# Rescheduling sparse expert visits and building part of the one-hot rows on ScalarE in a PEER encoder layer

## What is computed

```python
q = (ht @ w_q).reshape(T, PEER_HEADS, 2, PEER_HALF)          # 8 heads, two halves
s = jnp.einsum('thpd,hpnd->thpn', q, sub_keys)               # 128 keys for each half
... top 16 of 16 x 16 pairs for each head -> experts, gates  # 128 experts of 16,384 for each token
a = jax.nn.gelu(jnp.einsum('td,tkd->tk', xt, u[e]))
y = jnp.einsum('tk,tkd->td', g * a, v[e])
```

## Time and profile before

| | us |
|---|---|
| median of three runs (lowest to highest) | 2524.3 (2521.87 to 2529.54) |
| the profiled execution | 2519.59 |
| its span, first to last instruction | 2517.8 |
| PE busy | 2389.7 (95%) |
| DVE busy | 1828.6 (73%) |
| POOL busy | 1332.9 (53%) |
| ScalarE busy | 927.4 (37%) |

### The profile page before, as it was taken

The page is one execution under the profiler, slowest core; times in us unless marked ns, Lnnn a source line. Parts: engine busy times, 40 slices in busy tenths (PEclk is TensorE's granted clock), DMA queues, the critical chain, the costliest instruction groups (busy, mean ns, idle before and its releaser), DMA issues.

```text
span 2517.8 us, 34594 instructions
## 1 busy us (share of the span) xinstructions
PE 2389.7 (95%) x12777; PEld 2033.9 (81%) x12777; DVE 1828.6 (73%) x3571; ACT 927.4 (37%) x1426; POOL 1332.9 (53%) x892
## 2 busy tenths in 40 slices
PE   7988999999999898899999999899799999999997
PEld 7868999999866667788888888687688788878786
DVE  4673796454378788659897298597597688888886
ACT  4443444654333322333333333233233333333333
POOL 0000698000466674564444367588586388888860
PEclk9987999999999899999999999999999999999999
DMA  5433677877766665573444478978978899999994
GB/s 166 156 130 123 206 223 221 262 218 229 241 199 213 196 219 201 198 254 117 139 150 138 149 244 259 349 237 261 362 243 275 315 332 344 347 348 347 341 369 161
DMA packets 252679, 596.84 MB, mean 237 GB/s; under 512 B 35792, under 2 KB 118224, under 8 KB 251872
## 3 DMA queue, kind: packets, MB, share of 16 engines
q1 hardware_dynamic: 182496, 385.69, 45.8%
q0 software_dynamic: 67712, 201.61, 23.9%
q10 hardware_dynamic: 2304, 7.34, 0.9%
HBM read 521.12 MB, written 73.40 MB: 236 GB/s over the span
## 4 chain that ended last, share of the span: by engine, by line
PE 35%; POOL 17%; issue 4%; DMA 4%; DVE 4%; ACT 2%; SPq 1%; DVEq 0%; ACTq 0%
PE ps L805 28%; POOL a_got L478 9%; POOL picked L473 8%; PE ps L835 3%; DMA raw<-in_experts 3%; PE ps L1051 2%; DMA picked<-in_experts,vidx 1%; SPq L358 1%; DVE acc L1534 1%; DVE acc_odd L1534 1%; PE ps L1024 1%; POOL sp_lo L469 0%; PE ps L851 0%; ACT sp_hi L691 0%; DVE att L1317 0%
## 5 line engine op out<-in xcount | busy, mean ns | idle before, releaser
L473 POOL DMA_INDIRECT picked<-in_experts,vidx x384 | 517.7, 1348 | 542.6 <-PE ps L805 219.4
L805 PE MATMUL ps<-ht_hi,sp_hi 128*128 128x256 f32 (+1 forms) x2048 | 701.4, 342 | 17.4 <-DVE sp_lo L1583 14.4
L805 PE MATMUL ps<-ht_lo,sp_hi 128*128 128x256 f32 (+1 forms) x2048 | 690.4, 337 | 0.0
L805 PE MATMUL ps<-ht_hi,sp_lo 128*128 128x256 f32 (+1 forms) x2048 | 689.7, 337 | 0.0
L478 POOL DMA_INDIRECT a_got<-acts,aidx x384 | 514.9, 1341 | 127.5 <-issue 116.1
L469 POOL TENSOR_TENSOR sp_lo<-raw,sp_hi 128x1024 fp32r<-128x1024 f32 x112 | 296.9, 2666 | 453.0 <-ACT sp_hi L691 453.0
L805 PEld LDWEIGHTS ps<-ht_hi,sp_hi 128*128 128x128 f32 x2048 | 390.1, 190 | 61.4 <-DVE sp_lo L1583 19.1
L805 PEld LDWEIGHTS ps<-ht_hi,sp_lo 128*128 128x128 f32 x2048 | 389.5, 190 | 40.7
L805 PEld LDWEIGHTS ps<-ht_lo,sp_hi 128*128 128x128 f32 x2048 | 390.2, 191 | 36.4
L1583 DVE TENSOR_TENSOR sp_lo<-raw,sp_hi 128x1024 fp32r<-128x1024 f32 x144 | 176.3, 1224 | 223.1 <-ACT sp_hi L691 222.8
L699 ACT ACTIVATE act_g<-ps 128x256 f32<-128x256 f32 (+1 forms) x256 | 125.8, 491 | 527.2 <-PE ps L805 525.3
(11 more groups left out here) (187 smaller groups left out, 3608.2 us busy)
## 6 DMA issues: line engine op xcount, KB each, us to landing
raw<-in_experts SPq DMA_DIRECT2D x256, 512.0 KB, 3.9
v_raw<-in_experts SPq DMA_DIRECT2D x128, 512.0 KB, 5.9
raw<-in_front SPq DMA_DIRECT2D x104, 512.0 KB, 3.7
acts<-act_g SPq DMA_DIRECT2D x128, 256.0 KB, 3.3
act_in<-acts SPq DMA_DIRECT2D x128, 192.0 KB, 5.9
acts<-act_g SPq DMA_DIRECT2D x128, 128.0 KB, 2.2
gates<-stage SPq DMA_DIRECT2D x16, 1024.0 KB, 11.4
g_in<-gates SPq DMA_DIRECT2D x128, 128.0 KB, 5.9
```

Of the source, the lines that this page charges most:

```text
L473: pool.indirect_dma_start(picked[n % SLOTS][:, :], None, v_rows, bass.IndirectOffsetOnAxis(ap=vidx[:, n // P, n % P:n % P + 1], axis=0)).t ...
L805: last = pe.matmul(out, l, r, start=start and k == 0, stop=stop and k == 2, skip_group_check=True)
```

## The change

Four edits. ScalarE builds `hot_a` of each second group with two activations for each token, |iota - key| and then relu(gate - gate * that), which is the gate where the key matches and 0 elsewhere; PE waits for them with `hot_a_ready`. The list `weight` becomes 23 ahead of a gate step, 4 in a store step and 17 in others. The remainders of steps 181 to 183 go from POOL to DVE, and so the spread of visits begins at step 181. For a fourth row in `idx_t` (minus the gate) some buffers of the last phase get other addresses.

```diff
+TOP_K_END = N_KEYS + 53
...
-        idx_t = sb("idx_t", A0 + 16 * KB, [P, 3, SPARSE, P])
+        idx_t = sb("idx_t", A0 + 16 * KB, [P, 4, SPARSE, P])
...
-            if step < 56 or N_KEYS <= step < N_KEYS + 56:
+            if step < 56 or N_KEYS <= step < TOP_K_END:
                 by_pool[step] = len(by_pool) + 1
...
+            def hot_rows(t, g):
+
+                n = 32 * (t - SPARSE) + g
+                if n >= HOT:
+                    act.wait_ge(S["gate_mm"], n - HOT + 1)
+                act.wait_ge(S["idx_ready"], t - SPARSE + 1)
+                for k in range(4):
+                    tok = 4 * g + k
+                    last = act.activation(hot_a[:, g % HOT, k, :], s["iota"][:, :], ACT.Abs, scale=-1.0,
+                                          bias=idx_t[:, 0, t - SPARSE, tok:tok + 1])
+                last.then_inc(S["hot_dist"], 1)
+                act.wait_ge(S["hot_dist"], n // 2 + 1)
+                for k in range(4):
+                    tok = 4 * g + k
+                    last = act.activation(hot_a[:, g % HOT, k, :], hot_a[:, g % HOT, k, :], ACT.Relu,
+                                          scale=idx_t[:, 3, t - SPARSE, tok:tok + 1],
+                                          bias=idx_t[:, 2, t - SPARSE, tok:tok + 1])
+                last.then_inc(S["hot_a_ready"], 1)
...
                 gelu(step)
                 if step + 2 < STEPS:
                     u_hi(step + 2)
+                window = gate_window(step + 1)
+                if window:
+                    hot_rows(window[0], window[1] + 1)
...
                 pe.wait_ge(S["hot_ready"], n + 1)
+                if g % 2:
+                    pe.wait_ge(S["hot_a_ready"], n // 2 + 1)
...
-                dve.tensor_copy(idx_t[:, :, t - SPARSE, :], ps[:, 6, 0:3 * P].rearrange("p (c n) -> p c n", c=3)
-                                ).then_inc(S["idx_ready"], 1)
+                dve.tensor_copy(idx_t[:, 0:3, t - SPARSE, :], ps[:, 6, 0:3 * P].rearrange("p (c n) -> p c n", c=3))
+                dve.tensor_scalar(idx_t[:, 3, t - SPARSE, :], ps[:, 6, 2 * P:3 * P], -1.0, None, ALU.mult
+                                  ).then_inc(S["idx_ready"], 1)
...
-                for q in range(4):
-                    tok = 4 * g + q
-                    last = dve.tensor_scalar(hot_a[:, g % HOT, q, :], s["iota"][:, :], idx_t[:, 0, t - SPARSE, tok:tok + 1],
-                                             idx_t[:, 2, t - SPARSE, tok:tok + 1], ALU.is_equal, ALU.mult)
+                if g % 2 == 0:
+                    for q in range(4):
+                        tok = 4 * g + q
+                        last = dve.tensor_scalar(hot_a[:, g % HOT, q, :], s["iota"][:, :],
+                                                 idx_t[:, 0, t - SPARSE, tok:tok + 1],
+                                                 idx_t[:, 2, t - SPARSE, tok:tok + 1], ALU.is_equal, ALU.mult)
...
-            u_parts(N_KEYS + 56)
-            first_free = N_KEYS + 56
-            weight = [11 if gate_window(step + 1) else 8 for step in range(first_free, STEPS)]
+            u_parts(TOP_K_END)
+            first_free = TOP_K_END
+
+            def stores(step):
+                return any(0 <= step - GATES_AT[t] - GATE_ROWS < PARTS for t in DENSE[:-1])
+
+            weight = [23 if gate_window(step + 1) else 4 if stores(step) else 17 for step in range(first_free, STEPS)]
```

More of the change, by code:

```diff
@@ L181, in encoder_program @@
                   for i, at in enumerate((0, 4 * KB, 8 * KB, 12 * KB, V0 + 19 * KB + 512))]
-        v_raw = sb("v_raw", A0 + 32 * KB, [P, RING, 1024])
+        v_raw = [sb(f"v_raw{k}", A0 + at * KB, [P, 1024]) for k, at in enumerate((32, 36, 44, 28))]
         v_hi = [sb(f"v_hi{k}", A0 + at * KB, [P, 1024], F32R) for k, at in enumerate((0, 4, 48))]
         v_lo = [sb(f"v_lo{k}", A0 + at * KB, [P, 1024], F32R) for k, at in enumerate((8, 12, 60))]
-        act_in = [sb(f"act_in{k}", A0 + at * 512, [P, HALF]) for k, at in enumerate((42, 45, 112, 115))]
-        g_in = sb("g_in", A0 + 52 * KB, [P, RING, 2 * P])
+        act_in = [sb(f"act_in{k}", A0 + at * 512, [P, HALF]) for k, at in enumerate((104, 107, 112, 115))]
+        g_in = [sb(f"g_in{k}", A0 + at * KB, [P, 2 * P]) for k, at in enumerate((22, 23, 40, 41))]
         w_f = sb("w_f", 16 * KB, [P, 2, HALF])
@@ L210, in encoder_program @@
             "dve_step", "pool_step", "sc_done", "evac", "tk_first", "tk_second", "tk_diff", "tk_exp",
-            "tk_chosen", "idx_turned", "idx_ready", "hot_ready",
+            "tk_chosen", "idx_turned", "idx_ready", "hot_ready", "hot_dist", "hot_a_ready",
             "gate_mm", "gate_evac", "gate_out3", "gate_out4", "fg_in",
@@ L376, in load_v @@
             def load_v(r):
-                sp.dma_start(v_raw[:, r % RING, :], a["experts"][r, 1]).then_inc(v_in[r % RING], 16)
+                sp.dma_start(v_raw[r % RING][:, :], a["experts"][r, 1]).then_inc(v_in[r % RING], 16)
             def load_weights(r):
                 sp.dma_start(act_in[r % RING][:, :], acts_rows[1][r, :, P:]).then_inc(act_in_done[r % RING], 16)
-                sp.dma_start(g_in[:, r % RING, :], a["gates"][r, :, SPARSE * P:(NT - 1) * P]
+                sp.dma_start(g_in[r % RING][:, :], a["gates"][r, :, SPARSE * P:(NT - 1) * P]
                              ).then_inc(gate_in[r % RING], 16)
@@ L708, in v_part @@
                     act.wait_ge(S["y_done"], r - 2)
-                act.activation(v_hi[r % 3][:, :], v_raw[:, r % RING], ACT.Copy).then_inc(S["v_hi"], 1)
+                act.activation(v_hi[r % 3][:, :], v_raw[r % RING][:, :], ACT.Copy).then_inc(S["v_hi"], 1)
             def exponents(step):
@@ L1496, in hot @@
                     dve.wait_ge(S["gate_mm"], n - HOT + 1)
-                dve.tensor_tensor(hot_b[:, g % HOT], s["iota"][:, None, :].broadcast_to([P, 4, P]),
-                                  idx_t[:, 1, t - SPARSE, 4 * g:4 * g + 4, None].broadcast_to([P, 4, P]), ALU.is_equal)
-                for q in range(4):
-                    tok = 4 * g + q
-                    last = dve.tensor_scalar(hot_a[:, g % HOT, q, :], s["iota"][:, :], idx_t[:, 0, t - SPARSE, tok:tok + 1],
-                                             idx_t[:, 2, t - SPARSE, tok:tok + 1], ALU.is_equal, ALU.mult)
+                last = dve.tensor_tensor(hot_b[:, g % HOT], s["iota"][:, None, :].broadcast_to([P, 4, P]),
+                                         idx_t[:, 1, t - SPARSE, 4 * g:4 * g + 4, None].broadcast_to([P, 4, P]),
+                                         ALU.is_equal)
+                if g % 2 == 0:
[4 more added lines that the diff above has]
+                                                 idx_t[:, 2, t - SPARSE, tok:tok + 1], ALU.is_equal, ALU.mult)
                 last.then_inc(S["hot_ready"], 1)
@@ L1559, in weights @@
                 dve.tensor_tensor(w_f[:, r % 2, 2 * P:], act_in[r % RING][:, 2 * P:], stage[:, r, :], ALU.mult)
-                dve.tensor_tensor(w_f[:, r % 2, 0:2 * P], act_in[r % RING][:, 0:2 * P], g_in[:, r % RING], ALU.mult
+                dve.tensor_tensor(w_f[:, r % 2, 0:2 * P], act_in[r % RING][:, 0:2 * P], g_in[r % RING][:, :], ALU.mult
                                   ).then_inc(S["w_ready"], 1)
@@ L1573, in v_part @@
                     dve.wait_ge(S["a_done"], STEPS)
-                dve.tensor_tensor(v_lo[r % 3][:, :], v_raw[:, r % RING], v_hi[r % 3][:, :].bitcast(F32), ALU.subtract
+                dve.tensor_tensor(v_lo[r % 3][:, :], v_raw[r % RING][:, :], v_hi[r % 3][:, :].bitcast(F32), ALU.subtract
                                   ).then_inc(S["v_lo"], 1)
@@ L1658, in _ @@
                     u_parts(step + 1)
-                    hot(t, first)
+                    if step >= GATES_AT[SPARSE]:
+                        hot(t, first)
                     visits(min(share, 1))
-                    hot(t, first + 1)
+                    if step >= GATES_AT[SPARSE]:
+                        hot(t, first + 1)
                     visits(max(share - 1, 0))
```

## The result

| us | before | after |
|---|---|---|
| median of four runs (lowest to highest) | 2526.92 (2521.87 to 2534.59) | 2558.93 (2555.72 to 2559.49) |
| the profiled execution, its span | 2519.59, 2517.8 | 2558.72, 2556.9 |

The ratio is 1.0109 [1.008, 1.0138], so the kernel after is about 1% slower. The two profiled executions differ by 39.1 us, where the sum of the prediction gave 22.2.

The account below looks back on a forecast made before the run. PE was taken to set the pace in undisturbed stretches, with full DMA engines stalling store steps. The profiled 2519.6 - 35.4 + 57.6 gave 2541.8 us; from the median, 2524.3 + 22.2, about 2546 us, range 2513 to 2572.

Parts of the forecast that it names:

- ScalarE's late start: Gate steps: PE waits 1.2 us for ScalarE's rows in each of 48 steps, 57.6 us (33 to 68); chance 0.62.
- The chain: Gelu, rounding, four Abs, own wait, four Relu: reaches PE 3.89 to 4.62 us after the Gelu, wanted at +3.20.
- the upper bound: ScalarE's chain with extra operand at 0.113 us and SBUF read at 0.034: ends at 4.62 us, late by 1.42.
- the own wait: On ScalarE, between the Abs and the Relu: Relu waits 0.09 us for the engine's own semaphore.
- The win from the spread: Store steps with 0.40 instead of 1.51 visits: stall goes, 35.4 us won (bounds 20 to 38.4).
- The 4.7 us that I gave to POOL: Tile 4's gate steps, 209 to 224, before the change: 4.7 us lost to POOL's slower indirect DMAs.
- The gate step of DVE: DVE's work in a gate step: 6.8 us before, 6.1 after, both below PE's 7.25.
- its saving is worth nothing: DVE's saving in gate steps, 6.8 to 6.1 us, is worth nothing by itself because PE covers it.
- a choice between 7.5 and 9.1 us per step for POOL: POOL's issue of 2.29 visits per gate step: 7.5 us taken; 9.1 would make POOL the bound, 2578 us, chance 0.05.
- The small edits: Remainders moved to DVE, three more row operations, earlier fetching and moved buffers: together nothing, covered by idle time or slack.
- table loads: Rival in gate steps: Abs and Relu outside Gelu's table add two loads each, 123 us more, 2669; chance 0.01.
- the releaser's name at PE's second group: Sign in the profile: PE idle about 1.2 us ahead of each second group, ScalarE's Relu named as ending it.

Follow-up runs that it names:

- e2: The kernel after with DVE building all hot_a rows again, the new spread of visits kept: 2580.13 us, ratio 1.015 to the kernel before.
- e1: The kernel after with ScalarE's eight activations for step s + 1 issued before the Gelu of step s: 2517.95 us, ratio 0.9905 to the kernel before.
- e8: The kernel after with gates laid out in DRAM so stores write 8 KB runs instead of 512 B: 2548.93 us, ratio 1.0085 to the kernel before.
- e7: The kernel after with two loads of V moved from step 232 to step 240: one execution of 2557.84 us.
- e3: The kernel before with ScalarE building the second groups, old weights and old split of remainders kept: 2587.97 us, ratio 1.0177 to the kernel before.

## Why the prediction was right, and where it was off

**ScalarE's late start: right in mechanism and nearly in size.** Per step 1.16 us against 1.2. The chain reached PE at +4.46, inside 3.89 to 4.62. The Abs were as priced for the upper bound (0.293 apart against 0.29), the Relu a little cheaper (0.389 apart, 0.483 each, against 0.403 and 0.538), and the own wait 0.03 instead of 0.09. PE's load is late by 1.26 rather than 1.2, but the step behind it recovers 0.1. 48 steps are 55.7 us against 57.6. The Trainium skill ("ScalarE: Activation LUTs", What ACT_TABLE_LOAD costs) gave 387 and 480 ns and a chain of 4.48; these groups of the kernel after agree:

```profile
L717 ACT ACTIVATE hot_a<-hot_a,idx_t 128x128 f32<-128x128 f32 x60 | 24.7, 483 | 0.5
L711 ACT ACTIVATE hot_a<-iota,idx_t 128x128 f32<-128x128 f32 x60 | 19.0, 392 | 0.0
```

That page's Rules for kernel authors send relu to VectorE. DVE does make a row in less time here, in one operation of 0.350 us against two of 0.392 and 0.483 on ScalarE, but the time of the kernel did not follow from that: with the new spread, all rows on VectorE are 1.5% slower than the kernel before (e2), and half of them on ScalarE ahead of the Gelu 0.95% faster (e1). DVE's operation is no relu, so no run tests the rule itself.

**The win from the spread: the term that was mis-sized.** It was to be 35.4 us and was 19.6, just under its lower bound of 20. The range held because its upper end had been built with that bound. Three causes are seen.

- The rate. I divided 2.05 MB by 376 GB/s and found 5.4 us, level with PE. But 376 was measured with visits carrying a third of the bytes. With few visits, and the DMA share still full at 1.07, the traffic was 328 GB/s; an estimate from that is 6.2 us for 2.05 MB, over PE's 5.44. U falls behind slowly, and the debt shows at the end of the store stage. e8, with the same bytes and 391 GB/s in the queue that carries them, removes it in the first stage and leaves 2.6 us in the second. Bytes over busy time of that queue alone vary with the mix too: 336 GB/s by the earlier trace rows, 315 in the kernel after, and 320 in gate steps of the kernel before (1453 to 1560 us), where no gate is stored:

```profile
q1 hardware_dynamic: 4211, 11.42, 33.4%
```

- V. The issue of its first blocks takes SyncE 7.02 us ahead of step 234; moving them gave back 3 of that step's 16.32 us (e7, one execution).
- Tile 4. The 4.7 us that I gave to POOL went, though not by the spread: e3, with the old one, loses only 0.6 there (126.84 us from step 209 to 224). And 4.9 came from elsewhere: ScalarE waits around step 212, in the kernel after and at the same place in e7, for something that the profile doesn't show.

```profile
1668.62 0.60 ACT L785 ACTIVATE stage<-ps 128x512 f32<-128x512 f32 x1 [3.38 <-remote]
1672.21 0.60 ACT L700 ACTIVATE act_g<-ps 128x512 f32<-128x512 f32 x1 [3.00 <-remote]
```

```profile
1671.68 0.60 ACT L785 ACTIVATE stage<-ps 128x512 f32<-128x512 f32 x1 [3.36 <-remote]
1675.25 0.60 ACT L700 ACTIVATE act_g<-ps 128x512 f32<-128x512 f32 x1 [2.97 <-remote]
```

The first two rows are of the kernel after, the others of e7. The cause stays open. The profile of the kernel before has no such wait; e1 has some, at other steps.

**DVE and POOL.** The gate step of DVE was below PE's pace, as said. That its saving is worth nothing was wrong: it shortens no path of DVE's own, but beside the thinner DVE an issue takes POOL 1.04 us, where with all rows on DVE it takes 1.7 (e2). I had left a choice between 7.5 and 9.1 us per step for POOL and took the first because DVE is less dense; the choice was right (2.29 x (1.03 + 1.05 + 0.6) = 6.1 us in the kernel after), and e2 shows the other case, 2.29 x (1.76 + 1.63 + 0.6) = 9.1 us of POOL's work for a gate step.

**The rest.** The small edits were put at nothing. 2.15 us do come ahead of step 184's Gelu, but they stand already at the Gelu of step 128 (1146.24 us, 1144.09 before), ahead of all that was edited, so they are no cost of these edits; in the other kernels that Gelu starts at 1145.04 to 1156.64. No table loads were added. The clock, forecast at its higher level throughout, held in gate steps but for steps 213 and 234. Of the signs named, store steps of 5.4 to 5.6 us held except at the ends of the stages, and PE over 95% there held; the releaser's name at PE's second group did not, and the time for a block of U to land in the store steps is not in the profile after.

## What to carry to other kernels

Work that is moved to an idle engine is late or free by its place in that engine's queue: ask which event starts what stands ahead of it, and issue it before that event if its inputs allow. Rate a transfer by a stretch with the same mix of transfers: here the traffic fell from 376 to 328 GB/s as visits were taken out, with the DMA as full as before. Before calling an engine's saving worthless, look who slows down beside it.

## What was not expected of the hardware

- The queue of stores and U moved 315 GB/s with the stores in 512 B runs, and 391 with 8 KB runs (e8). The Trainium skill ("DMA: Bandwidth & Descriptors", Specifications) sets 512 B as the least transfer for the full rate; with runs just at that size the queue stayed under what it reached with long ones, and the measurement decides here. The loads of U in the same queue and the other addresses in e8 are not separated from that.
- An indirect DMA occupied POOL for 1.05 (`picked`) and 1.03 us (`a_got`) beside a DVE busy for 72% of the gate steps of tile 3, for 1.21 and 1.11 at 82% (e1), for 1.26 and 1.41 at 91% (the kernel before), and for 1.63 and 1.76 at 83% with DVE building every row (e2). Busy share alone does not order them; what DVE runs when the issue begins does more. In steps 184 to 255, issues that began while DVE ran nothing or `hot_a` took 0.95 to 0.96 us on average in each of these four kernels. Those that began in a visit, a remainder or `hot_b` took 1.71 in the kernel before, 1.14 in the kernel after, 1.40 in e1 and 1.99 in e2. One issue in e2 lasts until 0.82 us behind three such operations in a row:

```profile
1507.02 3.65 POOL L479 DMA_INDIRECT a_got<-acts,aidx  x1 [0.31 <-issue]
```

```profile
1506.84 1.28 DVE L1558 SCALAR_TENSOR_TENSOR acc_odd<-picked,wts,acc_odd 128x1024 f32<-128x1024 f32 x1
1508.04 1.22 DVE L1607 TENSOR_TENSOR sp_lo<-raw,sp_hi 128x1024 fp32r<-128x1024 f32 x1
1509.17 0.68 DVE L1518 TENSOR_TENSOR hot_b<-iota,idx_t 128x512 f32<-128x512 f32 x1
```

No run changed one of these operations alone, so this is an observation.
- Among the gate stores SyncE spent 3.70 us on the issue of a block of U and 7.02 on two of V, against 0.43 for a block of U right behind them. That a full queue holds it is the likely reading; how much the queue takes was not measured.
